# First attention of a hybrid decoder layer: values stationary in two column halves, gated in transposed form, copies shared by two engines

## The reference

```python
h = x @ w_in                                  # (qa, ka, va, ga, iq, ik, iw, c_q, c_kv, k_rope, gb)
# A: an indexer scores the keys, each query keeps its best 128 of the causal keys
att = einsum('bthd,btkhd->bhtk', qb, ks) * scale        # 8 heads of 64, rotated q and k
p = softmax(where(valid, att, -inf))
o = einsum('bhtk,btkhd->bthd', p, vs)
o_a = o * silu(ga)
# B: latent attention, 8 heads of 64 + 32, ordinary causal softmax, from low-rank q and kv
o_b = mla(c_q, c_kv, k_rope) * silu(gb)
out = concatenate([o_a, o_b]) @ w_out
x = layernorm(alpha * x + out)
```

## Time and profile before

| | us |
|---|---|
| median of 3 runs | 302.65 (302.54 to 302.68) |
| profiled execution, its own time | 303.14 |
| its span | 301.3 |
| TensorE busy | 292.1 (97%) |
| VectorE busy | 230.9 (77%) |
| GpSimd busy | 171.3 (57%) |
| ScalarE busy | 167.4 (56%) |
| input projection and preparation | to 174.0 |
| first attention, from the first steps with transposes | 174.0 to 209.4 |
| second attention with most of the output projection | 209.4 to 279.3 |
| rest of the projection, last layer norms, store | 279.3 to 301.3 |

### The profile page before, as it was taken

How to read it: one execution, slowest core, us unless ns; L and a number is a source line. 1 busy time by engine, 2 the same in 40 slices (tenths; PEclk the granted TensorE clock), 3 DMA queues, 4 the chain that set the end, 5 groups by cost and what they waited for, 6 DMA issues and landing times.

```text
span 301.3 us, 5146 instructions
## 1 busy us (share of the span) xinstructions
PE 292.1 (97%) x1634; PEld 251.9 (84%) x1634; DVE 230.9 (77%) x525; ACT 167.4 (56%) x405; POOL 171.3 (57%) x197
## 2 busy tenths in 40 slices
PE   8899999999999999999999999999999999999990
PEld 8899988888888888888888789999677788888890
DVE  2798987878999999997043653664998868977785
ACT  4764444585152262374358787788877786553200
POOL 5698957302999995635326788530494261817211
PEclk9999999999999999999999999999999999999997
DMA  7965552200244425320055577300950000030411
GB/s 238 324 185 166 156 163 71 70 2 0 76 136 139 138 77 141 100 70 2 0 139 147 215 197 175 110 2 23 347 191 0 2 0 2 36 107 0 141 70 70
DMA packets 19546, 31.84 MB, mean 106 GB/s; under 512 B 6496, under 2 KB 9056, under 8 KB 19520
## 3 DMA queue, kind: packets, MB, share of 16 engines
q1 hardware_dynamic: 19088, 31.35, 34.5%
q10 hardware_dynamic: 432, 0.18, 0.3%
HBM read 26.28 MB, written 2.10 MB: 94 GB/s over the span
## 4 chain that ended last, share of the span: by engine, by line
PE 93%; DMA 2%; DVE 2%; ACT 1%; issue 1%; SPq 0%; DVEq 0%; ACTq 0%
PE ps L1124 49%; PE ps L1427 15%; PE ps L1355 6%; PE ps L1371 5%; PE ps L1320 5%; PE ps L1386 3%; PE ps L1310 2%; DMA w_raw<-in_w_in 2%; PE ps L1313 2%; PE ps L1221 1%; PE ps L1139 1%; PE ps L1240 1%; PE ps L1400 1%; PE ps L1211 1%; DVE y_last L1038 0%
## 5 line engine op out<-in xcount | busy, mean ns | idle before, releaser
L470 POOL TENSOR_TENSOR w_lo<-w_raw,w_hi 128x512 fp32r<-128x512 f32 (+3 forms) x62 | 81.1, 1332 | 32.1 <-ACT w_hi L569 32.0
L1124 PE MATMUL ps<-w_hi,x_lo 128*128 128x512 f32 (+2 forms) x224 | 82.5, 371 | 0.0
L1124 PE MATMUL ps<-w_lo,x_hi 128*128 128x512 f32 (+2 forms) x224 | 82.5, 371 | 0.0
L569 ACT ACTIVATE w_hi<-w_raw 128x512 fp32r<-128x512 f32 (+3 forms) x62 | 35.9, 590 | 71.2 <-PE ps L1124 63.1
L1124 PE MATMUL ps<-w_hi,x_hi 128*128 128x512 f32 (+1 forms) x188 | 73.1, 389 | 0.0
L1124 PEld LDWEIGHTS ps<-w_hi,x_lo 128*128 128x128 f32 x224 | 42.1, 188 | 6.4
L1124 PEld LDWEIGHTS ps<-w_lo,x_hi 128*128 128x128 f32 x224 | 42.2, 188 | 5.9
L1427 PE MATMUL ps<-wo_hi,oT 128*128 128x512 f32 (+1 forms) x144 | 43.5, 372 | 0.0
L1124 PEld LDWEIGHTS ps<-w_hi,x_hi 128*128 128x128 f32 x188 | 35.3, 188 | 5.9
L688 ACT ACTIVATE probs<-probs,small 128x512 f32<-128x512 f32 (+3 forms) x64 | 35.7, 558 | 7.6 <-DVE small L951 7.1
L1355 PE MATMUL ps<-ident,probs 128*128 128x128 f32 x160 | 28.3, 274 | 0.4 <-ACT probs L688 0.2
(11 more groups left out here) (161 smaller groups left out, 555.7 us busy)
## 6 DMA issues: line engine op xcount, KB each, us to landing
w_raw<-in_w_in SPq DMA_DIRECT2D x20, 512.0 KB, 3.6
kaT_swap<-kaT SPq DMA_DIRECT2D x8, 256.0 KB, 3.7
w_raw<-in_w_out SPq DMA_DIRECT2D x4, 512.0 KB, 4.0
wo_early<-in_w_out SPq DMA_DIRECT2D x4, 512.0 KB, 5.4
wo_raw_b<-in_w_out SPq DMA_DIRECT2D x4, 512.0 KB, 5.2
x_res<-in_x SPq DMA_DIRECT2D x4, 512.0 KB, 7.4
x_raw<-in_xT SPq DMA_DIRECT2D x3, 512.0 KB, 7.9
out_y<-y SPq DMA_DIRECT2D x6, 256.0 KB, 2.2
```

The costliest lines, as they stand in the source:

```text
L470: pool.tensor_tensor(w_lo[:, s, 0:n], w_raw[:, s, 0:n], w_hi[:, s, 0:n], ALU.subtract).then_inc(w_lo_ready, 1)
L569: act.activation(dst, w_raw[:, s, 0:n], ACT.Copy).then_inc(w_hi_ready, 1)
L1124: ins = mm(dst, a, b, start=start and j == 0, stop=stop and j == len(pairs) - 1)
```

## The change

In the first attention the roles of the operands are exchanged. `outputs(u)` now works at odd heads only, for a pair of heads: 64 columns of `va` are stationary and 128 columns of `probsT` moving, and the two heads write partitions 0 to 63 and 64 to 127 of the same 128 columns of `ps_o`. The result is transposed: head and value dimension on the partitions, queries along the free axis. `probsT` gets four buffers.

The gate follows: `scale_gate(i)` on VectorE multiplies the gate by the reciprocal row sums (two steps after the block's last unit), `o_transposes(i, 0)` turns this gate two steps later, for all four blocks in the same way, and `gate_oaT(i)` copies the turned gate out of the slot into the gate's place and multiplies it by the PV bank. `copy_oT_hi` and `oT_low` read this product from SBUF, no longer from the slot.

Every second unit's probability copy (`DVE_COPY = 2`, odd units) is made by VectorE, the others by ScalarE, each with a semaphore of its own.

```diff
-    O_AFTER = [[NU_A + HEADS * (i + 1) + OT_AT - T_LAG + b for b in range(2)] for i in range(TT - 1)] + [[NU, NU]]
-    O_AFTER[0][0] = O_FIRST
+    O_AFTER = [[HEADS * (i + 1) + GATE_AT, NU_A + HEADS * (i + 1) + OT_AT - T_LAG + 1 if i < TT - 1 else NU] for i in range(TT)]
...
-    o_norm = sb("o_norm", 92, [P, A_WIDTH])
...
-    probsT = sb("probsT", 26, [P, 3, BANK])
+    probsT = sb("probsT", 24, [P, 4, BANK])
...
+        def by_dve(u):
+
+            return u < NU_A and u % DVE_COPY == DVE_COPY - 1
+
+        def wait_copied(eng, u):
+
+            n = sum(by_dve(w) for w in range(u + 1))
+            if by_dve(u):
+                eng.wait_ge(probsT_copied_dve, n)
+            else:
+                eng.wait_ge(probsT_copied, u + 1 - n)
+
+        def copy_free(eng, u):
+
+            if u < NU_A:
+                if u >= 4:
+                    eng.wait_ge(pv_done, u - 3)
+                return probsT[:, u % 4, 0:unit(u)[3]]
+            if u >= NU_A + 3:
+                eng.wait_ge(pv_done, u - 2)
+            return probsT_b[:, u % 3, 0, 0:unit(u)[3]]
+
+        def oaT(i):
+
+            return gate[:, ORDER[i], 0:A_WIDTH].rearrange("p (a b) -> p a b", a=4)
...
-            src = ps_pT[:, slot_of[i, b] % 2].rearrange("p (a b) -> p a b", a=4) if b == 0 else obT[:, :, :]
+            src = oaT(i) if b == 0 else obT[:, :, :]
...
                 if b == 0:
-                    act.wait_ge(transposed, n + 1)
-                    src = ps_pT[:, n % 2].rearrange("p (a b) -> p a b", a=4)
+                    act.wait_ge(o_ps_read, i + 1)
+                    src = oaT(i)
...
-                if u >= T_LAG:
+                if u >= T_LAG and not by_dve(u - T_LAG):
                     copy_probsT(u - T_LAG)
...
+            def copy_probsT(u):
+                dve.wait_ge(transposed, slot_of[u] + 1)
+                V.tensor_copy(copy_free(dve, u), ps_pT[:, slot_of[u] % 2, 0:unit(u)[3]]).then_inc(probsT_copied_dve, 1)
+
+            def scale_gate(i):
+
+                m = ORDER[i]
+                dve.wait_ge(probs_ready, HEADS * (i + 1))
+                wait_tok(dve, G_GA, m)
+                after(V.reciprocal(rinv, row_sum[:, HEADS * i:HEADS * (i + 1)]))
+                g3 = gate[:, m, 0:A_WIDTH].rearrange("p (h d) -> p h d", h=HEADS)
+                V.tensor_tensor(g3, g3, rinv.unsqueeze(2).broadcast_to([P, HEADS, A_DIM]), ALU.mult).then_inc(gate_a_scaled, 1)
+
+            def gate_oaT(i):
+
+
+                n, half = slot_of[i, 0], gate[:, ORDER[i], 0:A_WIDTH]
+                dve.wait_ge(transposed, n + 1)
+                V.tensor_copy(half, ps_pT[:, n % 2]).then_inc(gate_a_turned, 1)
+                dve.wait_ge(pv_done, HEADS * (i + 1))
+                dve.wait_ge(gate_a_turned, i + 1)
+                V.tensor_tensor(half, ps_o[:, i % 2], half, ALU.mult).then_inc(o_ps_read, 1)
...
+                if u >= T_LAG and by_dve(u - T_LAG):
+                    copy_probsT(u - T_LAG)
...
-                if 0 < v <= TT and j == PV_LAG and v != TT - 1:
-                    normalise(v - 1)
-                if 0 < v <= TT and j == PV_LAG + 1 and v != TT - 1:
-                    apply_gate(v - 1)
-                if u == NU_A:
-                    normalise(TT - 2)
-                if u == NU_A + 2:
-                    apply_gate(TT - 2)
+                if 0 < v <= TT and j == GATE_AT:
+                    scale_gate(v - 1)
+                if 0 < v <= TT and j == GATE_AT + T_LAG + 1:
+                    gate_oaT(v - 1)
...
-                    pe.wait_ge(*((oT_lo_ready, 2 * i + 1), (obT_ready, i + 1))[b])
+                    pe.wait_ge(*((gate_a_turned, i + 1), (obT_ready, i + 1))[b])
...
-                    if h == 0:
+                    if h % 2 == 0:
+                        return
+                    if h == 1:
...
-                    pe.wait_ge(probsT_copied, u + 1)
+
+                    for w in (u - 1, u):
+                        wait_copied(pe, w)
                     for j in range(m + 1):
-                        ins = mm(ps_o[:, v % 2, h * A_DIM:(h + 1) * A_DIM], probsT[:, u % 3, j * P:(j + 1) * P],
-                                 va[:, j, h * A_DIM:(h + 1) * A_DIM], start=(j == 0), stop=(j == m))
-                    ins.then_inc(pv_done, 1)
+                        for a in range(2):
+                            ins = mm(ps_o[A_DIM * a:A_DIM * (a + 1), v % 2, h // 2 * P:(h // 2 + 1) * P],
+                                     va[:, j, (h - 1 + a) * A_DIM:(h + a) * A_DIM],
+                                     probsT[:, (u - 1 + a) % 4, j * P:(j + 1) * P], start=(j == 0), stop=(j == m))
+                            if j == m:
+                                ins.then_inc(pv_done, 1)
                     return
...
-                    pe.wait_ge(o_ready, i + 1)
+                    pe.wait_ge(gate_a_scaled, i + 1)
...
-                if u == O_FIRST + T_LAG:
-                    o_transposes(0, 0)
-                if 0 < i < TT and OT_AT <= j < OT_AT + 2 and (i > 1 or j > OT_AT):
-                    o_transposes(i - 1, j - OT_AT)
+                for t in range(TT):
+                    if u == O_AFTER[t][0] + T_LAG:
+                        o_transposes(t, 0)
+                if 0 < i < TT and j == OT_AT + 1:
+                    o_transposes(i - 1, 1)
...
-            for b in range(2):
-                o_transposes(TT - 1, b)
+            o_transposes(TT - 1, 1)
...
+GATE_AT = 2
+DVE_COPY = 2
```

More of the change, by code:

```diff
@@ L251, in build @@
         scores_ready, masked_ready, probs_ready = sem("scores_ready"), sem("masked_ready"), sem("probs_ready")
-        transposed, probsT_copied = sem("transposed"), sem("probsT_copied")
+        transposed, probsT_copied, probsT_copied_dve = sem("transposed"), sem("probsT_copied"), sem("probsT_copied_dve")
         pv_done = sem("pv_done")
@@ L257, in build @@
         rinv_ready, gate_scaled, obT_ready = sem("rinv_ready"), sem("gate_scaled"), sem("obT_ready")
-        o_ps_read, o_ready = sem("o_ps_read"), sem("o_ready")
+        o_ps_read, gate_a_scaled, gate_a_turned = sem("o_ps_read"), sem("gate_a_scaled"), sem("gate_a_turned")
         oT_hi_ready, oT_lo_ready = sem("oT_hi_ready"), sem("oT_lo_ready")
@@ L704, in copy_probsT @@
                 act.wait_ge(transposed, slot_of[u] + 1)
-                if u >= 3:
-                    act.wait_ge(pv_done, u - 2)
-                dst = probsT[:, u % 3, 0:N] if u < NU_A else probsT_b[:, u % 3, 0, 0:N]
+                dst = copy_free(act, u)
                 act.activation(dst, ps_pT[:, slot_of[u] % 2, 0:N], ACT.Copy).then_inc(probsT_copied, 1)
             def copy_oT_hi(i, b):
-                n = slot_of[i, b]
                 if i == 0 and b == 0:
@@ L962, in _ @@
                         mask_unit(u)
[L964 to L975, removed]
-                wait_tok(dve, G_GA, m)
-                V.tensor_tensor(gate[:, m, cols], o_norm[:, :], gate[:, m, cols], ALU.mult).then_inc(o_ready, 1)
+            def copy_probsT(u):
[4 more added lines that the diff above has]
+                dve.wait_ge(probs_ready, HEADS * (i + 1))
+                wait_tok(dve, G_GA, m)
+                after(V.reciprocal(rinv, row_sum[:, HEADS * i:HEADS * (i + 1)]))
[8 more added lines that the diff above has]
+                V.tensor_tensor(half, ps_o[:, i % 2], half, ALU.mult).then_inc(o_ps_read, 1)
             def probs_low(u):
                 N, w = unit(u)[3], u % 3
-                dve.wait_ge(probsT_copied, u + 1)
+                wait_copied(dve, u)
                 V.tensor_tensor(probsT_b[:, w, 1, 0:N], ps_pT[:, slot_of[u] % 2, 0:N], probsT_b[:, w, 0, 0:N],
@@ L1001, in row_sums @@
                 dve.wait_ge(probs_ready, HEADS * (v + 1))
-                if v > TT:
+                if v == TT:
+                    dve.wait_ge(gate_a_scaled, TT)
+                else:
                     dve.wait_ge(gate_scaled, v - TT)
@@ L1342, in slot @@
                     i, b = slots[n - 2]
-                    pe.wait_ge(*((oT_lo_ready, 2 * i + 1), (obT_ready, i + 1))[b])
+                    pe.wait_ge(*((gate_a_turned, i + 1), (obT_ready, i + 1))[b])
                 elif slots[n - 2] < NU_A:
-                    pe.wait_ge(probsT_copied, slots[n - 2] + 1)
+                    wait_copied(pe, slots[n - 2])
                 else:
```

## The result

| | before | changed |
|---|---|---|
| median of 16 runs, us | 302.65 (302.12 to 303.62) | 303.32 (302.70 to 303.93) |
| ratio to before | 1 | 1.0021, 95% interval 1.0012 to 1.0029 |
| span of the profiled execution | 301.3 | 302.1 |

A forecast was written before the change was run, and what follows sets the result against it. TensorE was taken as the bound, with 93% of the chain. Halves together -4.8, entering +1.4 and VectorE's step +1.4 sum to -2.0 us: median 302.65 to 300.6 us, range 297.5 to 305.3.

The forecast's parts named there:

- Its own sign for that: First attention: the prediction is wrong in sign if products of probabilities and values (PV) take longer than 15.4 us in all.
- the other: Second attention: should keep its 69.9 us within 0.7; growing by more means the sum has missed a wait.
- Halves together: First attention's PV on TensorE: two heads' products stream at once in the array's column halves, 10.6 us against 15.4, gaining 4.8.
- the halves do not stream together: Rival for first attention's PV: 17.6 us against 15.4, together +2.6, total 305.3 us, up to 306.7; chance 0.21.
- Entering: TensorE, first attention: going into the half-array products 16 times at 0.09 us costs 1.4 us; bounds nothing and 2.9.
- VectorE's step: Turned gate's copy and product in one step make TensorE wait 1.6 us, net 1.4, bounds 0 and 2.4; fourth block nothing.
- Transposes that move: Gate transposes of blocks 1 to 3 move to earlier places; four cost 0.36 to 0.44 us anywhere, 0 in all.
- the tail: Behind the last PV: four transposes instead of eight; a start 0.4 us earlier leaves the ScalarE copy's wait hidden.
- step 18: ScalarE's copy_oT_hi(0, 0) waits for GpSimd's last w_out high part; with 3 us saved, still 1 us to spare, hidden.
- Copies: First attention: ScalarE loses 16 of 32 probability copies (7.0 us), worth little; VectorE gains 7.8 us, no bound by its mean.
- the halves stream together and the gain is eaten: Rival: entering and leaving at 2.9 and VectorE's step at 2.4 give +0.5, total 301.8 to 303.2 us; chance 0.14.

The follow-up runs named there:

- the serial order: The changed kernel with each head's products of a pair issued as one run, head outside and key tile inside: 305.22 us, ratio to before 1.0086.
- the version that beats both: Also "the candidate": changed kernel; GpSimd's late subtractions after last scale_gate, VectorE copies only odd units below 10, last gate one step earlier, block 0's low part at step 23: 300.72 us.

## Why the prediction was wrong

The measured 303.32 us lies in the stated range only because that range reached over the rivals that lose; the forecast of 2.0 us saved had the wrong sign. Its own sign for that, PV above 15.4 us in all, did not show (11.2), but the other did: the second attention grew by 1.9 us.

**Halves together: right.** The assumption that was to decide the sign held. 4.2 us measured, 4.8 forecast; the pairs came out 0.03 to 0.04 longer each. The rival "the halves do not stream together" is refuted. That the serial order measured 305.22 beside its 305.3 is a coincidence: the pairs took 14.2 us there and not the rival's 17.6.

**Entering: mis-sized by its base.** From the last four transposes to PV it is now 0.53 us (180.08 to 180.61), where four transposes before scores take 0.36: 0.17 for each of 16 entries, 2.7 us. But in the earlier trace rows the same step took 0.43, so 32 entries at 0.07 were already paid, 2.2 us. The net is about +0.5, not +1.4. The lower bound, nothing, was nearer than the term.

**VectorE's step: the failed one.** The prediction gave it 1.6 us of waits in the first three blocks, and for the fourth: "steps take 2.2 us and VectorE has work of normalise and apply_gate taken off: nothing". Measured were 2.5 and 2.1. Four things were missing.

- `scale_gate` was priced at 0.74 us by `apply_gate`, a product of two SBUF tiles like it. It took 0.99, 1.15, 0.69 and 1.78. The four instances of `apply_gate` took 0.69, 0.69, 0.79 and 0.81: two began with GpSimd idle, and two beside its subtractions lost little. The new place of the last `scale_gate` is where GpSimd starts its subtractions. A group in the trace of before had the warning: the same shape from SBUF, `x_lo`, with GpSimd subtracting beside most of its instances, at a mean of 1.09 us.

```profile
L789 DVE TENSOR_TENSOR x_lo<-x_raw,x_hi 128x512 fp32r<-128x512 f32 x8 | 8.5, 1086 | 3.3 <-ACT x_hi L594 3.2
```

- Moving a source from PSUM to SBUF changes who can block it. In the middle of the same GpSimd subtractions the subtraction of low parts at 217.55, with one source in PSUM, took its usual 0.68 us. `normalise` read PSUM, and so did `oT_low`; the changed `oT_low` of block 0 reads the product from SBUF and took 1.08 us, beside a subtraction, instead of 0.69 (with GpSimd quiet it took 0.69 from SBUF too, at 200.56 in the version that beats both). The prediction called it equal by leaving it out.
- The gate transposes of the last block stand at step 36 in the ring of two slots, and need unit 33's slot. In the kernel before, unit 35's transposes take that slot one step later. The prediction checked the slot that the gate's copy frees, and not the one that the gate's transposes need. VectorE frees it behind `scale_gate` in its queue, so this is how the slow product reaches TensorE: 1.15 us with a product of 1.78, 0.63 with one of 1.27, 0.05 with one of 0.69. In the first attention the same wait shows at step 20 (197.65).
- For the fourth block the prediction took VectorE's copy and product to fit into a step of 2.2 us. They start late in it, behind that step's mask and subtraction, and TensorE waited 0.37 and 0.45 us for them.

**Transposes that move, the tail, step 18: right.** 0.8 us and 0.4 us went from the late steps to the early ones, the tail lost at most 0.1 us of it (21.26 us from the first product behind the last gate transposes to the end, 21.16 before), and no exponential waited for the copy at step 18.

**Copies: half right.** That ScalarE's relief alone "is worth little" holds (0.9999 in the kernel before). That VectorE had room by its mean was true and beside the point: taking them back gave 0.6 us.

Of the rivals, "the halves stream together and the gain is eaten" is what happened, at 303.3 against its upper end of 303.2. Its mechanism is half of it: entering was not the eater, VectorE's queue was.

What stays open: about 1 us of waits is left at the entry of the candidate (16.99 us, against an estimate of 15.9 by the products alone: the 15.39 of before, 0.4 for the gate transposes, 0.14 for two pairs of one tile). Part of it is a wait of the gate transposes, now at step 35 (0.45 us). For the first attention no run takes GpSimd's work away from the slow products of blocks 0 and 1, so how the 2.5 us divide between collisions and the length of VectorE's queue is not shown. What the three untimed edits of the candidate gave each was not measured.

## What to carry to other kernels

When TensorE is 99% busy, less work for it pays only as far as the queues that feed it can follow; before pricing the gain, walk the slots in both directions: which one each new instruction frees, and which one it needs. Price an elementwise operation on VectorE by where its operands lie and what GpSimd does at that moment, not by shape: the same product took 0.69 and 1.78 us. And when a change gives back its gain, look at starts of a recurring instruction step by step: they showed two places of 2 us within a total that moved by 0.7.

## What the hardware showed that was not expected

- An 8-column product of two SBUF tiles on VectorE took 0.17 us alone and 1.27 us beside a GpSimd subtraction of 1.25 us; a 512-column one 0.69 and up to 1.78. It goes both ways: GpSimd's two subtractions at 195.09 took 2.96 us beside VectorE's product, where two take 2.5 otherwise. A subtraction with one source in PSUM took 0.68 us in the middle of GpSimd's.
- Plain f32 products, each of two records, overlap across the two column halves of the array: 16 records in 1.02 us when neighbours alternate, 1.51 us when each half's eight come in a run. For 8 records the order made no difference (0.59 us both ways), so the second head's records start beside the first head's even when four of the first stand before them. Entering from 128-column transposes costs 0.17 us; of leaving, 0.01 to 0.02 us show in the next score product, and a pair is 0.03 to 0.04 longer than its slots.
